# A two-layer hybrid trunk on one core: the hand-over between the layers, a third fixed expert, and where the routing tables are written

## The reference

```python
def trunk_layer(x, cond, lp, ...):
    sh1, sc1, g1, sh2, sc2, g2 = modulation(cond, lp['mod_w'], lp['mod_b'])
    mix, k, v, st = mixer(rms_norm(x, lp['norm1']) * (1 + sc1) + sh1, lp, ...)
    x = x + g1 * mix
    return x + g2 * hierarchical_moe(rms_norm(x, lp['norm2']) * (1 + sc2) + sh2, lp)

def hierarchical_moe(x, lp):
    # top 1 of 4 groups, then top 2 of the 8 gated MLPs (1024 -> 256 -> 1024) of that group
    y = grouped_expert_mlp(x, expert_idx, weights, lp['e_wg'], lp['e_wu'], lp['e_wd'])
```

## Time and profile before

| | |
|---|---|
| median of 3 runs (1494.43 to 1499.7) | 1497.56 us |
| profiled execution: its own time | 1498.07 us |
| its span, first to last instruction | 1496.3 us |
| mean granted clock of TensorE in it | 0.92 |
| HBM read and written | 322.41 and 27.61 MB |
| DMA rate over the span, mean | 224 GB/s |
| one tile of the weight stream | 1024 KB |

### The profile page before, as it was taken

How to read it: one execution, slowest core, us unless ns; L and a number is a source line. 1 busy time by engine, 2 the same in 40 slices (tenths; PEclk the granted TensorE clock), 3 DMA queues, 4 the chain that set the end, 5 groups by cost and what they waited for, 6 DMA issues and landing times.

```text
span 1496.3 us, 20523 instructions
## 1 busy us (share of the span) xinstructions
PE 1251.5 (84%) x7762; PEld 860.0 (57%) x7762; DVE 707.0 (47%) x1553; ACT 282.6 (19%) x708; POOL 113.4 (8%) x171
## 2 busy tenths in 40 slices
PE   5999999889977799879739999988798569988781
PEld 2765677557863455556337556766587345655450
DVE  2256866782356133223252686677444613333224
ACT  0211233651111000000022104256221100000000
POOL 2000000000001111111100000000100011111100
PEclk7999999999977999999969999999999569999896
DMA  9221101356058999999651110023913199999975
GB/s 386 108 88 57 57 1 57 120 197 269 29 197 357 414 419 420 420 416 412 244 225 54 63 57 29 1 84 150 367 71 113 49 416 419 418 420 418 405 293 225
DMA packets 58179, 334.61 MB, mean 224 GB/s; under 512 B 11392, under 2 KB 11392, under 8 KB 23900
## 3 DMA queue, kind: packets, MB, share of 16 engines
q1 hardware_dynamic: 42336, 294.94, 48.8%
q0 software_dynamic: 15744, 38.34, 6.6%
HBM read 322.41 MB, written 27.61 MB: 234 GB/s over the span
## 4 chain that ended last, share of the span: by engine, by line
PE 50%; DMA 21%; DVE 11%; SPq 7%; issue 4%; ACT 2%; DVEq 2%; PEld 1%; POOL 0%; ACTq 0%; PEldq 0%; POOLq 0%
PE bank L1616 12%; PE bank L1560 8%; DMA ring<-in_stream 8%; PE bank L1985 7%; PE bank L1875 7%; SPq L350 6%; DMA RAB<-in_stream 6%; PE bank L2019 5%; DMA mod_rows<-RAB 2%; DMA U<-in_stream 2%; DMA RAB<-mod_rows 2%; DMA U<-moe_out 1%; PE bank L1717 1%; PE bank L1891 1%; DVE U L1168 1%
## 5 line engine op out<-in xcount | busy, mean ns | idle before, releaser
L1985 PE MATMUL bank<-U,HT 128*64 128x256 f32 (+2 forms) x1088 | 205.4, 411 | 12.5 <-DMA RAB<-in_stream 4.7
L1985 PE MATMUL bank<-ring,HT 128*64 128x256 f32 (+2 forms) x736 | 143.3, 434 | 46.0 <-DMA RAB<-in_stream 27.7
L1616 PE MATMUL bank<-HT,ring 128*128 128x512 f32 (+1 forms) x640 | 175.4, 435 | 2.0 <-issue 2.0
L1985 PEld LDWEIGHTS bank<-U,HT 128*64 128x64 f32 (+2 forms) x1088 | 131.2, 154 | 51.0 <-issue 26.4
L1875 PE MATMUL bank<-ring,HT 128*128 128x256 f32 x640 | 148.7, 394 | 13.3 <-DVE U L1219 7.7
L1560 PE MATMUL bank<-ring,HT 128*128 128x256 f32 x640 | 149.1, 385 | 3.0 <-ACT HT L603 3.0
L1875 PEld LDWEIGHTS bank<-ring,HT 128*128 128x128 f32 x640 | 125.7, 199 | 33.0 <-issue 10.0
L1616 PEld LDWEIGHTS bank<-HT,ring 128*128 128x128 f32 x640 | 97.3, 191 | 79.7 <-issue 79.7
L1985 PEld LDWEIGHTS bank<-ring,HT 128*64 128x64 f32 (+2 forms) x736 | 85.6, 154 | 91.8 <-issue 70.9
L1560 PEld LDWEIGHTS bank<-ring,HT 128*128 128x128 f32 x640 | 119.4, 192 | 18.6 <-issue 3.7
L1008 DVE SCALAR_TENSOR_TENSOR U<-U,prm 128x655 f32<-128x655 f32 x120 | 107.8, 899 | 6.3 <-issue 0.4
(11 more groups left out here) (346 smaller groups left out, 1590.4 us busy)
## 6 DMA issues: line engine op xcount, KB each, us to landing
ring<-in_stream SPq DMA_DIRECT2D x162, 1024.0 KB, 18.7
U<-in_stream SPq DMA_DIRECT2D x90, 1024.0 KB, 28.0
RAB<-in_stream SPq DMA_DIRECT2D x14, 1024.0 KB
U<-moe_out SPq DMA_DIRECT2D x20, 512.0 KB, 7.6
RAB<-mod_rows POOLq DMA_DIRECT2D x12, 512.0 KB, 11.9
moe_in<-CAT POOLq DMA_DIRECT2D x10, 512.0 KB, 3.2
X<-in_x SPq DMA_DIRECT2D x1, 2560.0 KB, 15.0
out_y<-X SPq DMA_DIRECT2D x5, 512.0 KB, 6.9
```

Source lines behind the costliest of these rows:

```text
L1616: ins = e.matmul(out, wt(q)[:, k, P * (n % 2):P * (n % 2) + P], HT[:, k, lo:lo + w], start=(k == 0), stop=(k == KD - 1))
L1985: ins = e.matmul(PS[2 + p][s, FF * j:FF * j + FF], xgT[:, p, k, s], wt(key)[:, k, :], start=(k == 0), stop=(k == KD - 1))
```

## The change

1. `FIXED` is 3: expert 2 takes rank 2, and nine tiles (0 to 8) of the list need no table. `ROUNDS` is "PPFPFQBPBPPFBQBBPP" instead of "QFPPFBPPPBPBBQBBPP".
2. `lanes` is computed right behind the ranks, its steps set between those that follow them.
3. The router's tables and scratch lie in `HT`, whose normed rows have been used up by then, and not in `U` from `LATER` on. SP therefore loads tiles 9 to 12 right behind `lanes_rdy`; the waits for `wslot_ps` there and for `ov_go` go (the latter now stands ahead of the overflow test).
4. `place` in fp32 is a copy of `place16` by ACT (`place_rdy`), behind `slot_rdy`; DVE's second comparison (L1388) goes. PE waits for `place_rdy` ahead of the weight product, DVE ahead of `cmp`.
5. Between the layers the five tiles are taken as 0, then 1 and 2, then 3 and 4: adding the rows, squares, inverse root, scaling, turning and projecting follow one another by group, with PE, ACT and DVE each in a new hand-written order. In the last layer the rows are added as before.

The diff, without the lines that only rename or move an expression:

```diff
 FF = 256
-FIXED, BIGS, MIDS, SMALLS = 2, 8, 16, 8
+FIXED, BIGS, MIDS, SMALLS = 3, 8, 16, 8
 HALF, QUART = P // 2, P // 4
 NR = BIGS + MIDS // 2 + SMALLS // 4
 NOVF = 2 * NTOK // (HALF + 1)
 NBLK = NR + NOVF
 NOROW = 100000
 STATES = ((0, 0), (0, 1), (1, 0), (4, 1), (2, 0), (3, 1), (3, 0), (2, 1))
-ROUNDS = list("QFPPFBPPPBPBBQBBPP")
+ROUNDS = list("PPFPFQBPBPPFBQBBPP")


...
-        mt = view(LATER + 2 * D, 2, D)
-        place = view(LATER, 2 * NT, P)
-        blockno = view(LATER + 2 * NT * P, 2 * NT, NBLK)
-        rows16 = U[:, LATER + 2 * NT * (P + NBLK):LATER + 2 * NT * (P + 2 * NBLK)].bitcast(BF16).rearrange("p (j a n) -> p j a n", j=2 * NT, a=2)
-        place16 = U[:, LATER + 3 * D - NT * P:LATER + 3 * D].bitcast(BF16).rearrange("p (j n) -> p j n", j=2 * NT)
+        over = htf[:, 2 * D:3 * D].rearrange("p (e f) -> p e f", e=NE)
+        masked = htf[:, 3 * D:3 * D + 2 * NT * NE].rearrange("p (k t n) -> p k t n", k=2, t=NT)
+        cmp = htf[:, 2 * D:2 * D + NOVF * NE].rearrange("p (i n) -> p i n", i=NOVF)
+        place16 = htf[:, 2 * D:2 * D + NT * P].bitcast(BF16).rearrange("p (j n) -> p j n", j=2 * NT)
+        wblk = htf[:, 2 * D + NT * P:2 * D + NT * P + 2 * NT * NBLK].rearrange("p (j n) -> p j n", j=2 * NT)
+        place = htf[:, 0:2 * NT * P].rearrange("p (j n) -> p j n", j=2 * NT)
+        blockno = htf[:, 2 * NT * P:2 * NT * (P + NBLK)].rearrange("p (j n) -> p j n", j=2 * NT)
+        rows16 = htf[:, 2 * NT * (P + NBLK):2 * NT * (P + 2 * NBLK)].bitcast(BF16).rearrange("p (j a n) -> p j a n", j=2 * NT, a=2)
...
-                    load_expert(i)
-
-                e.wait_ge(S["ov_go"], l + 1)
-                e.wait_ge(S["wslot_ps"], l + 1)
-                for i in range(RING + EXT, PLACES - 1):
+                e.wait_ge(S["h2_rdy"], NT * (l + 1))
+                for i in range(3 * FIXED, PLACES - 1):
                     load_expert(i)
...
                 some = e.value_load(ovn[0:1, 0:1], min_val=0, max_val=NOVF)
...
-                normed_out(0)
-                normed_out(1)
-                for t in range(NT - 1):
-                    if t + 2 < NT:
+                def squares(t):
+
+                    e.wait_ge(S["x_rdy"], NT * (l - 1) + t + 1)
+                    A(nrow2, X[:, t, :], ACT.Square, accum_out=small(1400 + t, 1))
+                    e.drain()
+                    e.drain().then_inc(S["sq_rdy"], 1)
+
+                if l:
+                    squares(0)
+                    normed_out(0)
+                    for t in range(1, 4):
+                        squares(t)
+                    qkv_out(0)
+                    normed_out(1)
+                    normed_out(2)
+                    squares(4)
+                    qkv_out(1)
+                    qkv_out(2)
+                    normed_out(3)
+                    normed_out(4)
+                else:
+                    normed_out(0)
+                    normed_out(1)
+                    for t in range(NT - 2):
                         qkv_out(t)
...
                 A(small(1220, NT), small(1220, NT), ACT.Exp).then_inc(S["soft_y"], 1)
-                for j in range(1, modd(l) // 2):
+                for j in range(1, before_slots(l)):
                     parts_out(l, 1, j, MODBANK[j])
+                e.wait_ge(S["slot_rdy"], l + 1)
+                A(place, place16, ACT.Copy).then_inc(S["place_rdy"], 1)
+                for j in range(before_slots(l), modd(l) // 2):
+                    parts_out(l, 1, j, MODBANK[j])
+
...

-                if l + 1 < DEPTH:
-                    for t in range(NT):
-                        e.wait_ge(S["x_rdy"], NT * l + t + 1)
-                        A(nrow2, X[:, t, :], ACT.Square, accum_out=small(1400 + t, 1))
-                        e.drain()
...

+                def norm1(t0, n):
+
+                    e.wait_ge(S["sq_rdy"], (3 + NT) * l - NT + t0 + n)
+                    rs(n, 1.0 / D, 1400 + t0)
+
                 if l:
-                    e.wait_ge(S["sq_rdy"], 4 * l)
-                    rs(NT, 1.0 / D)
-                    scaled(0)
-                    scaled(1)
+                    rows_back(0, l - 1)
...

-                for t in range(NT):
-                    evac1(t)
-                    if t + 2 < NT:
-                        scaled(t + 2)
+                if l:
+                    norm1(0, 1)
+                    scaled(0)
+                    rows_back(1, l - 1)
+                    evac1(0)
+                    rows_back(2, l - 1)
+                    rows_back(3, l - 1)
+                    norm1(1, 2)
+                    scaled(1)
+                    scaled(2)
+                    evac1(1)
+                    evac1(2)
+                    rows_back(4, l - 1)
+                    norm1(3, 2)
+                    scaled(3)
+                    scaled(4)
+                    evac1(3)
+                    evac1(4)
+                else:
+                    for t in range(NT):
+                        evac1(t)
+                        if t + 2 < NT:
+                            scaled(t + 2)
...

-                    e.wait_ge(S["sq_rdy"], 4 * l + signal)
...
-                e.memset(key[:, 0:1], 1e6)
-                e.memset(key[:, 1:2], 1e6 - 1)
+                for n in range(FIXED):
+                    e.memset(key[:, n:n + 1], 1e6 - n)
                 e.scalar_tensor_tensor(out=key[:, FIXED:], in0=cnt[:, FIXED:], scalar=float(NE), in1=iota[:, FIXED:NE],
                                        op0=ALU.mult, op1=ALU.subtract); dr()
-                over = mt[:, 1, :].rearrange("p (e f) -> p e f", e=NE)
                 e.tensor_tensor(over, key.unsqueeze(1).to_broadcast((P, NE, NE)), key.unsqueeze(2).to_broadcast((P, NE, NE)), ALU.is_gt); dr()
                 e.tensor_reduce(rank, over, AX, ALU.add); dr()
+                lane = small(1279, 1)
+                e.tensor_scalar(key, rank, rowno[:, 0, 0:1], -1.0, ALU.subtract, ALU.is_equal)
                 e.tensor_scalar(capm, rank, float(BIGS), float(HALF), ALU.is_lt, ALU.mult)
                 e.tensor_scalar(step, rank, float(BIGS + MIDS), float(QUART), ALU.is_lt, ALU.mult)
                 e.scalar_tensor_tensor(out=at0, in0=rank, scalar=float(BIGS + MIDS), in1=rank, op0=ALU.min, op1=ALU.add)
                 e.tensor_scalar(small(1660, NE), rank, float(BIGS), 2.0, ALU.min, ALU.mult); dr()
+                e.tensor_tensor_reduce(small(1280, NE), key, iota[:, 0:NE], 1.0, 0.0, ALU.mult, ALU.add, lane)
                 e.tensor_tensor(capm, capm, step, ALU.add)
                 e.tensor_tensor(at0, at0, small(1660, NE), ALU.add); dr()
-                e.tensor_scalar(at0, at0, float(QUART), None, ALU.mult)
+                e.tensor_scalar(lane, lane, 3.0, float(experts(l)), ALU.mult, ALU.add)
+                e.tensor_scalar(at0, at0, float(QUART), None, ALU.mult); dr()
+                e.tensor_copy(lanes[:], lane).then_inc(S["lanes_rdy"], 1)
...

-                lane = small(1279, 1)
-                e.tensor_scalar(key, rank, rowno[:, 0, 0:1], -1.0, ALU.subtract, ALU.is_equal); dr()
-                e.tensor_tensor_reduce(capm, key, iota[:, 0:NE], 1.0, 0.0, ALU.mult, ALU.add, lane); dr()
-                e.tensor_scalar(lane, lane, 3.0, float(experts(l)), ALU.mult, ALU.add); dr()
-                e.tensor_copy(lanes[:], lane).then_inc(S["lanes_rdy"], 1)
...
                 e.tensor_copy(gidx[:], sf).then_inc(S["gidx_rdy"], 1)
-                e.tensor_tensor(place, iota[:].unsqueeze(1).to_broadcast((P, 2 * NT, P)),
-                                small(160, 2 * NT).unsqueeze(2).to_broadcast((P, 2 * NT, P)), ALU.is_equal)
...
                     modulation(l, j)
-                ovf, cmp = small(1662, 1 + NOVF), mt[:, 1, 0:NOVF * NE].rearrange("p (i n) -> p i n", i=NOVF)
...

-                for t in range(NT):
-                    e.wait_ge(yld[t], 32 * (l + 1))
+                def rows_back(t, m):
+
+                    e.wait_ge(yld[t], 32 * (m + 1))
                     e.tensor_tensor(X[:, t, :], X[:, t, :], yk[0][:, t, :], ALU.add); dr()
                     e.tensor_tensor(X[:, t, :], X[:, t, :], yk[1][:, t, :], ALU.add).then_inc(S["x_rdy"], 1)
+
+                if l + 1 == DEPTH:
+                    for t in range(NT):
+                        rows_back(t, l)

...

+                arrived(b)
+                arrived(b + 1)
                 if l:
                     normed_tile(l, 0)
+                    qkv_tile(0)
                     normed_tile(l, 1)
-                arrived(b)
-                arrived(b + 1)
-                for t in range(NT - 1):
-                    qkv_tile(t)
-                    if t + 2 < NT:
-                        normed_tile(l, t + 2)
+                    normed_tile(l, 2)
+                    qkv_tile(1)
+                    qkv_tile(2)
+                    normed_tile(l, 3)
+                    normed_tile(l, 4)
+                    qkv_tile(3)
+                else:
+                    for t in range(NT - 1):
+                        qkv_tile(t)
```

(3 more changed lines are left out.)

12 lines of the change are left out of this document (7 added, 5 removed).

## The result

The changed kernel takes 1487.34 us (median of 8 runs), the kernel before 1497.78 us beside it (8 runs). The ratio is 0.9921 (95% interval 0.9901 to 0.9941), so 11.8 us less (8.8 to 14.8). Four runs of that series have a median of 1483.39 beside 1498.91 before: ratio 0.9894 (0.986 to 0.9929), 15.9 us less (10.6 to 21.0).

A forecast was written before the change was run, and what follows sets the result against it. The experts were taken as bound by the DMA stream: when it runs without a gap and the bytes left then. Gains 9.5 + 0.8 + 5.5 = 15.8 us from 1498.07, 0.5 less for the median, gave 1482 us, range 1476 to 1490.

The forecast's parts named there:

- the forecast itself: Whole kernel: the main case, a gain of 12.5 to 20 us, given a chance of 0.6.
- rival A: Layer 1 experts: gathers' 8.5 us are their own price, not the queue's; part gains 4.5, total 1487 us; chance 0.17.
- Experts of layer 1: Early loads take 24.6 us of transfers out, the stream restarts 15 us later; gain 9.5 us.
- The hole: Layer 1: stream has nothing to do from 1194 until buffers come free; gapless from about 1208.
- I take 3: Layer 1: the row gather lands 3 us behind its issue, taken from layer 0's last scatter, 2.96 us.
- Experts of layer 0: Tile 6 fills a gap in the stream, less small delays; gain 0.8 us, bounds -1 and 2.5.
- The dent: Layer 0: stream at only 147 GB/s over 466 to 468; tile 6 fills it, 2.5 us.
- Hand-over: Between the layers: tile 0's projection starts 10.4 us earlier, the fourth ends 5.7 earlier; gain taken as 5.5 us.
- The worry over the clock: Between the layers: projection 0 wholly at half clock takes 14.2 us instead of 7.1, leaving 0.3 us of gain.
- B: Between the layers: clock or DVE's new order leaves 0.3 to 2 us instead of 5.5; total 1486 us; chance 0.1.
- C: Both layers: third fixed expert starves the first rounds, 21 us a layer, total 1524 us; chance 0.05, including overflow.
- D: Whole kernel: no effect, within 4.5 us, as a bound elsewhere takes the time back; chance 0.05.

The follow-up runs named there:

- a_full: The changed kernel run once more for a profile at the usual clock; median 1483.39 us over four runs, ratio 0.9894 to the kernel before.
- c_experts: The changed kernel with the old order of work between the layers; 1487.04 us, ratio 0.9941 to the kernel before.
- j_warm_hand: The changed kernel with 15 unread PE products before tile 0's turning between layers, tile 3's additions behind copies of tiles 1 and 2; 1482.44 us, ratio 0.9882.
- b_between: The kernel before with only the new order of work between the layers; 1493.6 us, ratio 0.9963 to the kernel before.
- d_fixed2: The changed kernel with two fixed experts and the old order of rounds; 1487.83 us, ratio 0.9924 to the kernel before.
- e_lanes_late: The changed kernel with the table of ranks (`lanes`) computed behind `slot_rdy` again, as before; 1491.52 us, ratio 0.9936 to the kernel before.
- the two halves: Two runs: the new order between the layers alone on the kernel before (1493.6 us), and the changed kernel without it (1487.04 us).

## Why the prediction was right

The forecast was 1482 us (1476 to 1490) and the measurement 1487.34, in the range but outside the 12.5 to 20 us of gain that I had given the forecast itself; the gain is 11.8 us of the 15.8 in the sum. That the time falls on rival A's 1487 is chance: A's mechanism is not what the runs show. The stages let each term be checked:

- **Experts of layer 1: 9.5 forecast.** 287.7 us (mean of `a_full`, `c_experts`, `j_warm_hand`, whose code there is the same) against 296.4 (before and `b_between`): 8.7 gained, by the last load 8.9 (256.6 less 247.7). Tiles left as forecast: table at 1180.70 (1181.5 forecast), tiles 9 to 12 from about 1181.6 (1182.4). The hole was longer: restart 34.2 us behind the rank product instead of 32.5 (1208 less 1175.55). By the sum of the prediction that leaves 7.8; the further 0.9 us is within what this stage scatters by (286.0 to 289.0 in the kernels with three fixed experts and the early table). The step that was mis-sized is "I take 3" for the gather, from the scatter's 2.96: it takes 5.4, and the store 4.5 instead of 3. Of these 2.4 us more, 1.4 reach PE (turning 24.7 us behind the rank product, 23.3 forecast), the others lie beside the weight product; the gate products took 6.5 us where I had 5.5.
- **Experts of layer 0: 0.8 forecast.** 299.0 against 299.9, 0.9 gained, but this stage scatters by more (297.6 to 300.9 over the changed kernels), so the term is neither borne out nor refuted. The dent is filled, as said.
- **Hand-over: 5.5 forecast.** 52.2 (mean of eight) against 57.5 (before and `c_experts`): 5.3 gained. Start of projection 0 forecast at 765.3, measured 765.41; small products 800.4 and 801.62. The worry over the clock was half right: projection 0 took 10.08, not 7.1, but DVE's tile 1 was due at 774.1 anyway (turned at 775.34, as projection 0 ends), so 3 us of slow clock cost about 1.
- The three terms measured make 8.7 + 0.9 + 5.3 = 14.9 us, above the 11.8 of the first comparison (at the upper edge of its interval) and below the 15.9 of the second. The rest lies, in the one profile there is, in stages that the change leaves alone: `a_full` lost 3.7 us of its lead in the output projection of layer 1 (92.1 us, 88.4 before). For the runs of the first comparison, which have no profile in the usual state, this is not shown.
- **Rival A** falls as a mechanism, by `a_full`, `d_fixed2` and `e_lanes_late`: 5.4 us with an idle stream, 9.5 to 10.4 with tiles left. I had argued for it from the Trainium skill ("DMA: Bandwidth & Descriptors", section "Queues, rings and completion order"), by which a DMA engine takes turns between its queues packet by packet. The trace agrees with that once the gather runs (83 packets of either queue over 1204 to 1206 in `e_lanes_late`), but it does not follow that the price is the gather's own: a gather that shares the engines is slower, and its first packet came 2.5 us later. The 7.9 us that I read as a minimum price contained stream in every case: 2.1 to 3.1 MB of SP's loads ran in the first 7.9 us of each of the 36 gathers.
- **B** (clock or DVE's order) was a loss of 1 us, not of 3.5 to 5.2. **C** did not occur: the DMA share is 1.00 over the opening rounds, 1209 to 1239. **D** falls by the two halves.
- A reason that I had not given: the third fixed expert does not pay by its three tiles as such. In `d_fixed2` as in `a_full` all 14 buffers are filled ahead of the restart, and from there to the last load it is 213.3 and 213.6 us, so the same bytes are left. It pays because its tiles have been moved when the gather is issued: with two fixed experts, and tiles still on the way then, the gather takes 4.4 us more, the gates start 32.1 us behind the rank product, as before the change (31.6), and the restart comes 4 us later.

## What to carry over

Where a stream is bounded by bytes, look for the stretch in which its queue waits for a table, and move loads there; then look at the first small transfer behind them, since here the loads still running beside it (5.4 us alone, 9.5 to 10.4 with them) set when the engines begin to return buffers. The best place for moved loads is early enough to have drained when the gather is issued. When parts are worth 1 us to 5 us in a kernel whose untouched stages vary by up to 7 us, compare stages between fixed instructions and not totals.
